# Down projection of a decoder layer: second chunk's activations read earlier into another buffer, gate rows read one a chunk, embedding rows turned in the tenth chunk

## The reference

```python
up, ffn_state = causal_dwconv(rms_norm(x, g_pre_ffn) @ w_up, ffn_prev, w_conv_f, b_conv_f)
gate, val = jnp.split(up, 2, axis=-1)                       # each 2816 wide
x = x + rms_norm((jax.nn.gelu(gate) * val) @ w_down, g_post_ffn)
e = (p @ w_ple) * jax.nn.sigmoid(rms_norm(x, g_ple_gate) @ w_ple_gate)
x = x + rms_norm(e, g_post_ple)
```

## Time and profile before

| what | us |
|---|---|
| median of 3 runs | 1752.1 |
| the three runs | 1751.03, 1756.45, 1752.1 |
| the profiled execution, its own time | 1753.01 |
| its span, first to last instruction | 1751.3 |
| TensorE busy in the span | 1720.7 (98%) |
| VectorE busy | 1101.7 (63%) |
| ScalarE busy | 739.6 (42%) |
| GpSimd busy | 337.0 (19%) |
| mean granted clock of TensorE | 0.993 |

### The profile page before, as it was taken

How to read it: one execution, slowest core, us unless ns; L and a number is a source line. 1 busy time by engine, 2 the same in 40 slices (tenths; PEclk the granted TensorE clock), 3 DMA queues, 4 the chain that set the end, 5 groups by cost and what they waited for, 6 DMA issues and landing times.

```text
span 1751.3 us, 28014 instructions
## 1 busy us (share of the span) xinstructions
PE 1720.7 (98%) x9496; PEld 1500.6 (86%) x9496; DVE 1101.7 (63%) x1538; ACT 739.6 (42%) x1302; POOL 337.0 (19%) x273
## 2 busy tenths in 40 slices
PE   9999999999999999999799999999999799999998
PEld 8989998998999899988688888888888688888886
DVE  6364155326514556657688888888887677667566
ACT  6445244434524452234544444444444511113665
POOL 1000000000000000004356666666661300000200
PEclk9999999999999999999999999999999899999999
DMA  5312321131232134343222222222233432222343
GB/s 170 98 53 71 89 68 61 54 103 52 67 88 60 47 113 145 129 159 116 66 64 77 77 77 77 77 77 77 76 101 114 161 100 100 93 78 99 108 139 114
DMA packets 166111, 161.91 MB, mean 92 GB/s; under 512 B 12511, under 2 KB 140859, under 8 KB 166012
## 3 DMA queue, kind: packets, MB, share of 16 engines
q1 hardware_dynamic: 155066, 155.76, 27.5%
q10 hardware_dynamic: 10946, 4.91, 1.0%
HBM read 121.01 MB, written 39.62 MB: 92 GB/s over the span
## 4 chain that ended last, share of the span: by engine, by line
PE 96%; DVE 1%; ACT 1%; issue 1%; DMA 1%; SPq 0%; ACTq 0%; DVEq 0%
PE pair L2867 11%; PE pair L2562 10%; PE pair L2564 9%; PE pair L2563 9%; PE pair L2927 8%; PE pair L2928 8%; PE pair L2929 8%; PE pair L3049 5%; PE pair L2516 5%; PE pair L3050 5%; PE pair L3052 4%; PE pair L2936 2%; PE pair L2738 2%; PE pair L2708 2%; PE pair L2493 2%; PE pair L2491 2%
## 5 line engine op out<-in xcount | busy, mean ns | idle before, releaser
L2562 PE MATMUL pair<-xh,wh 128*128 128x384 f32 (+1 forms) x952 | 329.7, 346 | 0.0
L2564 PE MATMUL pair<-xh,wl 128*128 128x384 f32 (+1 forms) x952 | 311.4, 327 | 0.0
L2563 PE MATMUL pair<-xl,wh 128*128 128x384 f32 (+1 forms) x952 | 311.0, 327 | 0.0
L2562 PEld LDWEIGHTS pair<-xh,wh 128*128 128x128 f32 x952 | 179.0, 188 | 14.2 <-issue 11.5
L2563 PEld LDWEIGHTS pair<-xl,wh 128*128 128x128 f32 x952 | 179.5, 189 | 0.0
L2564 PEld LDWEIGHTS pair<-xh,wl 128*128 128x128 f32 x952 | 178.8, 188 | 0.0
L940 POOL TENSOR_TENSOR srow<-hn,hn 128x512 f32<-128x512 f32 x8 | 13.8, 1725 | 812.6 <-DVE hn L2131 812.3
L3049 PE MATMUL pair<-wh,f 128*128 128x512 f32 x396 | 156.0, 394 | 8.3 <-DVE y L2285 7.4
L3050 PE MATMUL pair<-wl,f 128*128 128x512 f32 x396 | 155.3, 392 | 0.0
L2287 DVE TENSOR_TENSOR y<-y,pair 128x512 f32<-128x512 f32 x160 | 108.5, 685 | 58.2 <-PE pair L3052 58.2
L3052 PE MATMUL pair<-wh,f 128*128 128x512 f32 x352 | 138.0, 392 | 0.0
(11 more groups left out here) (383 smaller groups left out, 4192.1 us busy)
## 6 DMA issues: line engine op xcount, KB each, us to landing
rawp<-in_w_up SPq DMA_DIRECT2D x88, 256.0 KB, 3.6
raw<-in_w_in SPq DMA_DIRECT2D x80, 256.0 KB, 3.2
f_spill<-cv SPq DMA_DIRECT2D x22, 552.0 KB, 2.8
fraw<-f_spill SPq DMA_DIRECT2D x22, 552.0 KB, 6.5
raw<-in_w_down SPq DMA_DIRECT2D x44, 256.0 KB, 2.9
gat<-gate_spill SPq DMA_DIRECT2D x16, 544.0 KB, 4.5
x_spill<-x SPq DMA_DIRECT2D x16, 512.0 KB, 2.9
gate_spill<-stg SPq DMA_DIRECT2D x32, 192.0 KB, 1.9
```

Of the source, the lines that this page charges most:

```text
L2562: t_.matmul(b, h, xhi, start=(k == 0), stop=False, skip_group_check=True)
L2563: t_.matmul(b, h, xlo, start=False, stop=False, skip_group_check=True)
L2564: ins = t_.matmul(b, l, xhi, start=False, stop=(k == KD - 1), skip_group_check=True)
```

## The change

- fraw1, the raw buffer of odd chunks, moves from over ug and uv to low memory; pn takes its former place; u2 and u3 move 640 bytes up, out of fraw1's way.
- SP loads chunk 1's activations after spill(20, 0), once the last pair's weights are split; chunk 1's weights are loaded earlier as well. SP's loop over the chunks is written out. Gate rows go out one a chunk in chunks 0 to 5, pn in chunk 6, g_ffn and g_ple in chunk 7.
- ScalarE makes gate_high(0) to (5) one a chunk in chunks 2 to 7, behind the first weight half; its loop is written out too.
- p_turned, p_high and p_low go to chunk 9: TensorE behind units 0, 3, 6, 9, 12 and 15, VectorE behind units 1, 4, 7, 10, 13 and 16, ScalarE three behind the activations and three behind the next weight half.

```diff
--- before.py
+++ after.py
@@ -197,7 +197,7 @@
         ph, pl = a.take("ph", [P, 2, TOK], F32R), a.take("pl", [P, 2, TOK], F32R)
         y_last = at("y_last", [P, D], 163840)
         x2h = at("x2h", [P, BLK, KD, P], R1 + 17408, F32R)
-        pn = at("pn", [P, BLK + 1, PLE], LOW)
+        pn = at("pn", [P, BLK + 1, PLE], 202240)
         wgate = [[at(f"wg{n}{k}", [P, D], (R2 + k * 8192 if k < 6 else R1 + (k - 6) * 8192) + 4096 * i, F32R)
                   for i, n in enumerate("hl")] for k in range(KD)]
         wraw = [at(f"wgr{k}", [P, D], R2 + k * 8192 + 4096) for k in range(6)]
@@ -283,7 +283,7 @@
         a = Region(R3T, RTOP)
         f1 = a.take("f1", [P, 2, 2 * TOK], F32R)
         fb = [f2, f1]
-        fraw = [a.take("fraw0", [P, 2, UPC]), at("fraw1", [P, 2, UPC], 202240)]
+        fraw = [a.take("fraw0", [P, 2, UPC]), at("fraw1", [P, 2, UPC], LOW)]
 
         rawp = [at("rawp0", [P, 2, KD, P], R3), at("rawp1", [P, 2, KD, P], LOW)]
         adh, adl = (at(n, [P, 2, KD, P], R3 + 8192 * (i + 1), F32R) for i, n in enumerate(("adh", "adl")))
@@ -296,7 +296,7 @@
             (LOW, LOW + 2048, LOW + 4096), (LOW + 6144, LOW + 12288, 172800), (163840, 165888, 170752),
             (R3T + 12288, R3T + 14336, R3T + 4096)))]
         o_fold = at("o_fold", [P, D], LOW + 8192)
-        u2, u3 = at("u2", [P, HALF], LOW + 8192), at("u3", [P, HALF], LOW + 10240)
+        u2, u3 = at("u2", [P, HALF], LOW + 8832), at("u3", [P, HALF], LOW + 10880)
         sb = at("sb", [P, 2, P], LOW + 14336)
         a = Region(R3T, RTOP)
         cg = a.take("cg", [P, UPC])
@@ -817,40 +817,40 @@
             spill(19, 1)
             hold(d_f, 22)
             spill(20, 0)
-            hold(p_q, 8 * NFF)
-            for k in range(6):
-                sp.dma_start(wraw[k][:, :], w_gate[:, k:k + 1, :].rearrange("p o n -> p (o n)")).then_inc(gate_in[k], 16)
-            sp.dma_start(gains[:, :], inp["g_ple_gate"].rearrange("l (k p) -> p (l k)", p=P), allow_slow_non_contiguous=True).then_inc(gains_in, 16)
+            hold(d_ul, 4 * 22)
+            f_landed(1)
+            f_rows(1, 1)
+            hold(d_dl, 1)
+            down_rows(1, 0)
             hold(d_f, 23)
             spill(21, 1)
-            hold(d_q, 5 * NFF)
-            sp.dma_start(pn[:, 0:BLK, :], pp).then_inc(p_in, 16)
-            sp.dma_start(pn[0:NS, BLK, :], psm).then_inc(p_in, 16)
-            hold(d_cv, NFF)
-            hold(g_so, NFF)
-            f_landed(1)
-            f_rows(1, 1)
-            broadcast(g_ffn, "g_post_ffn", g_in[1])
-            broadcast(g_ple, "g_post_ple", g_in[2])
-
-            c2 = Count()
-
-            def down_body(t, s, f_too=True):
-
-                for h in range(2):
-                    hold(d_dl, c2.at(h + 1))
-                    down_rows(t + 1, h)
-                if f_too:
-                    hold(d_fl, c2.at(2))
-                    f_rows(t + 2, s)
-                c2.step(2)
-
-            f_landed(NCH - 1)
-            down_body(0, 0)
-            with loop(sp, 4, {c2: 4}) as t:
-                for j in range(2):
-                    down_body(t * 2 + 1 + j, (1 + j) % 2)
-            down_body(9, 1, False)
+            hold(d_dl, 2)
+            down_rows(1, 1)
+            sp.dma_start(gains[:, :], inp["g_ple_gate"].rearrange("l (k p) -> p (l k)", p=P), allow_slow_non_contiguous=True).then_inc(gains_in, 16)
+
+            def gate_rows(k):
+                sp.dma_start(wraw[k][:, :], w_gate[:, k:k + 1, :].rearrange("p o n -> p (o n)")).then_inc(gate_in[k], 16)
+
+            for t in range(NCH - 1):
+                if t:
+                    for h in range(2):
+                        hold(d_dl, 2 * t + h + 1)
+                        down_rows(t + 1, h)
+                if t < NCH - 2:
+                    f_landed(t + 2)
+                    hold(d_fl, 2 * t + 2)
+                    f_rows(t + 2, t % 2)
+                if t < 6:
+                    if t == 0:
+                        hold(p_q, 8 * NFF)
+                    gate_rows(t)
+                if t == 6:
+                    hold(a_st, NFF + 1)
+                    sp.dma_start(pn[:, 0:BLK, :], pp).then_inc(p_in, 16)
+                    sp.dma_start(pn[0:NS, BLK, :], psm).then_inc(p_in, 16)
+                if t == 7:
+                    broadcast(g_ffn, "g_post_ffn", g_in[1])
+                    broadcast(g_ple, "g_post_ple", g_in[2])
             for i in range(2):
                 hold(x1_out[i], 16 * ((NBK - i + 1) // 2))
 
@@ -1626,16 +1626,11 @@
                 then(s_.activation(raw_, raw_, ACT.Copy, scale=gains[:, k:k + 1]))
                 s_.activation(wgate[k][0][:, :], raw_, ACT.Copy).then_inc(a_gh, 1)
 
-            for k in range(3):
-                gate_high(k)
             for s in range(2):
                 act.wait_ge(f_out[s], F_OUT0 + 16 * 12)
-            c18, c32 = Count(), Count()
             for j in range(2):
                 f_high_in(1, j, 32)
             down_high(64, 0, NBK, p_dn)
-            c18.step(UNITS)
-            c32.step(32)
 
             def p_high(i):
 
@@ -1644,29 +1639,19 @@
                 w = GROUPS[gr][1]
                 s_.activation(part(ph[:, k, :], gr), turn[:, i % 2 * 512:i % 2 * 512 + w], ACT.Copy).then_inc(a_ph, 1)
 
-            for i in range(2 * NG):
+            for t in range(1, NCH - 1):
+                down_high(32 * t + 32, 1, UNITS * t, p_dn)
+                for j in range(2):
+                    f_high_in((t + 1) % 2, j, 32 * ((t + 1) // 2 + 1))
+                if t == NCH - 2:
+                    for i in range(3):
+                        p_high(i)
+                down_high(32 * t + 64, 0, UNITS * t + NBK, p_dn)
+                if 2 <= t < 8:
+                    gate_high(t - 2)
+            for i in range(3, 2 * NG):
                 p_high(i)
-            for k in range(3, 6):
-                gate_high(k)
-
-            c16 = Count()
-            c16.step(16)
-
-            def down_body(t):
-
-                down_high(c32.at(32), 1, c18.at(), p_dn)
-                for j in range(2):
-                    f_high_in((t + 1) % 2, j, c16.at(32 if t % 2 == 0 else 48))
-                down_high(c32.at(64), 0, c18.at(NBK), p_dn)
-                c18.step(UNITS)
-                c32.step(32)
-                c16.step(16)
-
-            with loop(act, 4, {c18: 2 * UNITS, c32: 64, c16: 32}):
-                down_body(1)
-                down_body(2)
-            down_body(9)
-            down_high(c32.at(32), 1, c18.at(), p_dn)
+            down_high(32 * NCH, 1, UNITS * (NCH - 1), p_dn)
 
             def gate_last(k, turn_):
 
@@ -2321,16 +2306,18 @@
                     if b in (4, 7):
                         f_low_in((t + 1) % 2, b // 6, c4.at(3 + b // 6))
                     down_unit(b, b, 0)
+                    if t == 9 and b % 3 == 1:
+                        p_low(b // 3)
                 for b in range(NBK):
                     if b == 2:
                         down_low(0, c2.at(3))
                     down_unit(NBK + b, b, 1)
+                    if t == 9 and b % 3 == 1:
+                        p_low(3 + b // 3)
                 c18.step(UNITS)
                 c2.step(2)
                 c4.step(2)
 
-            for i in range(2 * NG):
-                p_low(i)
             with loop(dve, 4, {c18: 2 * UNITS, c2: 4, c4: 4}):
                 down_body(1)
                 down_body(2)
@@ -3091,11 +3078,11 @@
                     for b in range(NBK):
                         u = NBK * h + b
                         down_unit(fb[t % 2], u, b, h, c18.at(u - 5))
+                        if t == 9 and u % 3 == 0:
+                            p_turned(u // 3)
                 c18.step(UNITS)
                 c2.step(2)
 
-            for i in range(2 * NG):
-                p_turned(i)
             with loop(pe, 4, {c18: 2 * UNITS, c2: 4}):
                 down_body(1)
                 down_body(2)
```

## The result

The changed kernel takes 1738.3 us (median of 4 runs, 1738.09 to 1738.95) against 1753.07 us for the kernel before in the same comparison (4 runs, 1751.03 to 1756.45): ratio 0.9918, 95% interval 0.9906 to 0.9929. In a later comparison (5 runs against 9) it measured 1738.43 against 1751.4, ratio 0.9925 (0.9912 to 0.9939). It is faster by 0.8%. The profiled execution took 1738.95 us, its span is 1737.2 us, 14.1 less than before.

The account below looks back on a forecast made before the run. TensorE was taken as the bound, with idle and half-speed time around the first two chunks to win. Gain 15.97 - 2.0 = 14.0 us from the median 1752.1 gave 1738.1 us, range 1736.0 to 1744.0.

Parts of the forecast that it names:

- The stall goes with 0.4 us to spare: TensorE's 7.6 us wait at chunk 0's unit 15 vanishes: evacuation lets it start at 1361.54, bank needed at 1361.95.
- rival A: Last spill before chunk 1's activations takes 9.3 us, not 3.4; unit 15 4.3 us late, 1744.0 us; chance 0.06.
- Its causes: Gate rows ahead on ScalarE and late-loaded activations together hold up chunk 1's activations, stalling TensorE 7.6 us at unit 15.
- The sum from the stall to chunk 2: Unit 15 of chunk 0 to chunk 2's start: 43.17 us before, 27.20 after, gain 15.97 us.
- The half speed in it: Halved TensorE clock behind the stall, 1.60 us, and behind the transposes, 2.23 with a short wait; both gone.
- 18 x 0.11 = 2.0 us: Cost of the 18 embedding transposes moved to chunk 9, all on TensorE's path, at 0.11 us each.
- rival C: Clock falls in chunk 9 among the transposes: one fall 1740.3 us, all six 1751; chances 0.04 and 0.02.
- Gate rows one a chunk: Chunks 2 to 7: GpSimd's gate step may make VectorE up to 2.3 us late six times; covered, cost nothing.
- The cover of 3.5 us in banks: Chunks 2 to 7: unit 11's evacuation done at 1542.4, TensorE needs that bank for unit 17 at 1545.9.
- Loop entry, loads, moved addresses: TensorE's loop entry straight from matmuls taken as 0, at most 0.74 us; spread-out loads and moved buffers cost nothing.
- 14.0 worked out: Whole forecast gain in us: 15.97 from stall to chunk 2, less 2.0 for the transposes in chunk 9.
- the second fall: TensorE at half speed a second time, behind the embedding transposes at chunk 1's start; 2.23 us with a short wait.

Follow-up runs that it names:

- the run with both edits: Changed kernel with three gate rows again ahead of chunk 1's activations and the 18 transposes again between chunks 0 and 1; 1750.77 us, single run.

## Why the prediction was right

The forecast was 1738.1 us, the range 1736.0 to 1744.0; measured 1738.3. Point by point:

- **The stall goes with 0.4 us to spare: right.** Counted from the start of chunk 0, unit 15 starts after 20.23 us, as in the kernel before without the stall (1361.95 - 1341.72). VectorE's evacuation begins at 1359.80; plus the 0.74 us from there to TensorE's start that is 1360.54, with 0.56 us to spare instead of 0.41, since ScalarE's activations began 15.15 us after chunk 0's start instead of 15.32. The last spill landed 3.8 us after its issue, at 1355.4, ahead of 1356.02: rival A did not occur.
- **Its causes.** The working named gate rows and load together. The runs part them: the gate rows alone make all of it; the load alone makes 2.36 us where the edit puts it, and an estimated 5.8 us in its place of before. So either of these two parts of the change by itself would have left most of the stall: 7.41 us measured with only the load moved, 5.8 estimated with only the gate rows moved.
- **The sum from the stall to chunk 2: right**, 15.97 worked out and 15.91 measured. The half speed in it (1.60, and most of 2.23) was rightly taken as gone with the stall. That short stalls pay the same was not known: rival A's price, length plus 1.6, happened to have that form.
- **Transposes: the term that was mis-sized.** "18 x 0.11 = 2.0 us" measured 2.75. The row it was priced by, eight full transposes in one group, had one change from transposes to matmuls where chunk 9 has six, and no 64-row form. Four groups cost 0.37 each, two cost 0.63; with full size in all, 25.74 - 23.58 = 2.16 are left, 0.12 each. So 0.59 of the missing 0.75 us is the 64-row form, and 0.16 is left for the smaller groups, which were not tried by themselves.
- **The clock in chunk 9 (rival C): right to doubt it.** It is 1.00 with 18 transposes among the matmuls, and in the run with all of them between the chunks, 1.9 us of waits included. By the Trainium skill (TensorE: Matmul & The Clock Gate, Part 4) transposes don't count as busy time; no run here shows a fall that they brought about by themselves, and the kernel before and the run with both edits show one behind them when a long stall preceded.
- **Gate rows one a chunk: cost right, picture wrong.** The forecast had VectorE's weight subtraction stretched; it came first by 10 ns and GpSimd stretched instead. The cover of 3.5 us in banks held either way. The Trainium skill (SBUF — State Buffer, Who interferes with whom) says that issue order decides who blocks; the two timelines agree, 3.48 and 2.95 us.
- **Loop entry, loads, moved addresses: nothing**, as taken. TensorE is busy for 212.00 of 212 us.
- **The error of 0.75 us** in the transposes is hidden in the whole time by the start, which was 0.85 us faster in the profiled execution. So 14.0 worked out against 13.2 measured from chunk 0 on is the fair comparison, and that the whole time was met within 0.2 us is luck: against the four runs' median of the kernel before, 1753.07, the gain is 14.8.

What stays open: why the second fall needs the stall ahead of it, and whether it is the transposes or the waits between them (0.85 and 0.71 us) that it follows. The runs show that both edits together bring it, not by what rule.

## What to carry to other kernels

When an engine stalls in a fixed order of work, list all that stands ahead of the late instruction on each engine that feeds it, loads included, and give each its own finish time: the second cause shows in no wait while the first covers it, and removing only the first would by the estimate above have won under 2 of the 7.6 us. A stall of TensorE cost more here than its length, because of the half speed behind it, down to the shortest one tried (2.36 us). Work that only has to be done some time (gate rows here) is free where banks cover it. Small edits are judged in the trace from a fixed point near them, since the start alone scatters by more than they bring.

## What was not expected of the hardware

- Half speed followed stalls of 2.4, 2.8 and 7.4 us alike and cost 1.75, 1.77 and 1.44 us. Behind the waits among the transposes (0.93 and 0.71 us), without a stall ahead, it did not come, nor behind the gap of 0.81 us ahead of chunk 0.
- A transpose of 64 rows between two full ones and a matmul cost TensorE 0.27 us more than a full one of 128 in its place. Eight such in a row, in the last stage, took 0.84 us, eight full ones 0.89 (distances between the matmuls around them, less the matmuls). The changed kernel's rows of these, the 64-row ones first:

```profile
1695.34 0.71 PE L2503 MATMUL pair<-ident,x 64*128 64x64 f32 x8
```

```profile
1708.38 1.04 PE L2503 MATMUL pair<-ident,x 128*128 128x128 f32 x8
```

  So the 64-row transpose isn't dear in itself, and the change of shape is the likelier cause; that was not tried by itself.
- In the first 100 us, where the code is the same, TensorE's busy time differed by up to 3.7 us from execution to execution (93.77 and 97.47).
